# Feature-major products with a wider moving operand, and a 512-token job run inside the modulation's load

## What is computed

```python
# first block: x, ctx are 256 x 2048 each
sh, sc, gt = split(silu(c) @ w_ada + b_ada, 3)        # and the same of c_ctx
h_x = rms_norm(x, norm_g) * (1 + sc_x) + sh_x
h_c = rms_norm(ctx, norm_g) * (1 + sc_c) + sh_c
px, pc = split_cols(h_x @ w_in), split_cols(h_c @ w_in)   # w_in 2048 x 6976
# four attention mixers, w_out, x + gt_x * (...)
# second block
z, xbc, dt, q, k, v = split(rms_norm(h, g) @ w_in_2)      # xbc: 3072 columns
xbc = silu(causal_dwconv(xbc, conv_w))                    # 4 taps along the tokens
# state space and window attention, w_out_2
u = causal_dwconv(rms_norm(h, g) @ w_up, ffn_conv_w)      # 3 taps, 2 x 5632 columns
h = h + (silu(g_ff) * u_ff) @ w_down
# per-layer gate and projection
```

## Time and profile before

| | us |
|---|---|
| median of 3 runs | 2368.04 (2367.92 to 2368.23) |
| the profiled execution | 2368.59 |
| its span, first to last instruction | 2366.8 |
| TensorE busy | 2253.2 |
| VectorE busy | 1397.2 |
| ScalarE busy | 989.5 |

### The profile page before, as it was taken

One profiled execution on the slowest core, in us unless ns is written; L12 is line 12 of the kernel. 1 busy time (PEld: TensorE's weight loads), 2 busy tenths in 40 slices (PEclk: granted clock), 3 DMA queues, 4 the chain that ended last, 5 costly groups with the idle time before them and its releaser, 6 DMA issues.

```text
span 2366.8 us, 33302 instructions
## 1 busy us (share of the span) xinstructions
PE 2253.2 (95%) x13134; PEld 1927.9 (81%) x13134; DVE 1397.2 (59%) x1955; ACT 989.5 (42%) x1413; POOL 110.8 (5%) x106
## 2 busy tenths in 40 slices
PE   5899999998799899999989999999999999999998
PEld 1387888996568788998759888899999999788877
DVE  1357565634745577676566544667767776544465
ACT  1333232334544444444456544444444443344453
POOL 1000000002300021000000000000000000000000
PEclk8999999999899999999989999999999999999999
DMA  9975565543025466556400466556565665666554
GB/s 367 348 217 167 186 213 169 152 128 93 1 71 187 138 187 192 175 183 199 142 1 1 147 202 195 149 174 186 178 194 169 185 184 165 205 194 192 194 165 164
DMA packets 209084, 399.86 MB, mean 169 GB/s; under 512 B 15257, under 2 KB 23965, under 8 KB 208012
## 3 DMA queue, kind: packets, MB, share of 16 engines
q1 hardware_dynamic: 205520, 386.71, 51.9%
q0 software_dynamic: 2160, 7.20, 1.3%
q10 hardware_dynamic: 1292, 4.41, 0.5%
HBM read 395.25 MB, written 3.01 MB: 168 GB/s over the span
## 4 chain that ended last, share of the span: by engine, by line
PE 86%; DVE 6%; DMA 4%; ACT 2%; issue 1%; POOL 1%; SPq 0%; DVEq 0%; ACTq 0%
PE bank L1765 51%; PE bank L1776 27%; DMA ada_ring<-in_w_ada 4%; PE bank L1878 1%; PE bank L2046 1%; PE bank L1939 1%; PE bank L1861 1%; PE bank L1928 1%; PE bank L2059 1%; DVE wlo L1079 1%; PE bank L1870 0%; PE bank L1930 0%; POOL st L570 0%; PE bank L1905 0%; ACT kt L677 0%
## 5 line engine op out<-in xcount | busy, mean ns | idle before, releaser
L1079 DVE TENSOR_TENSOR wlo<-raw,whi 128x1024 fp32r<-128x1024 f32 (+2 forms) x649 | 773.5, 1204 | 584.7 <-ACT whi L670 570.3
L670 ACT ACTIVATE whi<-raw 128x1024 fp32r<-128x1024 f32 (+2 forms) x649 | 669.6, 1045 | 858.8 <-PE bank L1765 413.2
L1765 PE MATMUL bank<-whi,xl 128*128 128x512 f32 (+2 forms) x1904 | 734.0, 386 | 20.1 <-DVE wlo L1079 10.0
L1765 PE MATMUL bank<-whi,xh 128*128 128x512 f32 (+2 forms) x1904 | 728.4, 383 | 0.0
L1765 PE MATMUL bank<-wlo,xh 128*128 128x512 f32 (+2 forms) x1904 | 728.2, 382 | 0.0
L1776 PE MATMUL bank<-xl,whi 128*128 128x256 f32 x1792 | 507.9, 283 | 0.3 <-DVE xl L1128 0.3
L1776 PE MATMUL bank<-xh,wlo 128*128 128x256 f32 x1792 | 507.3, 283 | 0.0
L1776 PE MATMUL bank<-xh,whi 128*128 128x256 f32 x1792 | 507.2, 283 | 0.0
L1765 PEld LDWEIGHTS bank<-whi,xl 128*128 128x128 f32 x1904 | 359.1, 189 | 93.9 <-DVE wlo L1079 12.5
L1765 PEld LDWEIGHTS bank<-wlo,xh 128*128 128x128 f32 x1904 | 359.2, 189 | 68.7
L1765 PEld LDWEIGHTS bank<-whi,xh 128*128 128x128 f32 x1904 | 359.3, 189 | 65.7
(11 more groups left out here) (310 smaller groups left out, 1570.5 us busy)
## 6 DMA issues: line engine op xcount, KB each, us to landing
raw<-in_w_in SPq DMA_DIRECT2D x216, 512.0 KB, 4.4
raw<-in_w_up SPq DMA_DIRECT2D x176, 512.0 KB, 3.7
raw<-in_w_out SPq DMA_DIRECT2D x96, 512.0 KB, 4.6
raw<-in_w_down SPq DMA_DIRECT2D x88, 512.0 KB, 4.8
ada_ring<-in_w_ada SPq DMA_DIRECT2D x64, 512.0 KB, 11.6
gate_w<-in_w_ada SPq DMA_DIRECT2D x32, 512.0 KB, 3.9
raw<-in_w_ple_gate SPq DMA_DIRECT2D x32, 512.0 KB, 4.9
raw<-in_w_in SPq DMA_DIRECT2D x16, 384.0 KB, 3.3
```

Source lines behind the costliest of these rows:

```text
L670: nc.scalar.activation(whi[:, slot, 0:size], raw[:, slot, 0:size], ACT.Copy).then_inc(hi_ready, 1)
L1079: tt_(wlo[:, slot, 0:size], raw[:, slot, 0:size], whi[:, slot, 0:size].bitcast(F32), ALU.subtract).then_inc(lo_ready, 1)
L1765: ins = mm(b4[tt][:, 0:width], x[:, o:o + P], w, start=k == 0 and i == 0, stop=k == last and i == 2)
```

## The change

It has four parts.

**Wide feature-major products.** `XH` and `XL` are now the two halves of one tensor `XHL`. One matmul has `whi` as stationary operand and both 256-token halves moving (512 columns, two pieces 15360 floats apart), and fills the whole bank: high x high in the first half, high x low in the second. A second one adds low x high to the second half. ACT copies the second half of each bank (`low_half`, `UX` for the up projection), DVE adds the first half (`whole`) and releases the banks; the taps read the sum in SBUF. The parts stand a step later in the lists. For `xbc` the first tap goes to ACT.

**Input tiles inside the modulation's load.** Jobs 0 and 1 change places: job 0 is now one with 24 products a tile. Its first six tiles are loaded after modulation tiles 8, 10, 24, 26, 40 and 42, split at 13, 14, 29, 30, 45 and 46, and multiplied after 18, 23, 34, 39, 50 and 55. Behind the load come two tiles of job 1, the last two of job 0, and the rest in order. The ring of modulation tiles has nine slots, outside the weight ring, and one bank.

**Rounds untied from tiles.** PE transposes for four rounds after modulation tiles 14, 15, 17 and 18 (and 16, 32 later), two banks in turn; ACT and DVE finish them after 16 to 19. The column products move from tile 18 to tile 15. x and ctx are loaded ahead of the gain rows, and x is normalised ahead of ctx.

**Gate tiles and the tail.** The first eight gate tiles move to every second tile of 16 to 30 (jobs 2 and 3, 12 products a tile). Behind the up projection ACT splits nine tiles before its last high part, and DVE has a split between each two parts.

The core of the diff:

```diff
-ADA_RING = 12
+ADA_RING = 9
...
+        XHL = at("xhl", 12288, [P, 2, 15360], FR)
+        XH, XL = XHL[:, 0, :], XHL[:, 1, :]
...
-        MOD = at("mod_rows", 35840, [P, 2 * D])
-        ADA = at("ada_ring", 0, [P, ADA_RING, 1024])
+        MOD = at("mod_rows", 35840, [P, 4, W])
+        ADA = [at(f"ada_ring{i}", o, [P, 1024]) for i, o in enumerate(
+            (24576, 25600, 26624, 37888, 38912, 39936, 40960, 41984, 49984))]
...
+        UX = at("up_x", 51032, [P, 4, 256])
...
-        X_ROUND = {27 + 2 * k + 6 * (k // 4): k for k in range(12)}
-        MOD_COLS = {16 * i + 18: i for i in range(3)}
+        MOD_COLS = {16 * i + 15: i for i in range(3)}
+        X_ROUND = {16 * (k // 4) + 16 + k % 4: k for k in range(12)}
+        X_TURN = {16 * (k // 4) + (14, 15, 17, 18)[k % 4]: k for k in range(12)}
+        IN1_LOAD = {16 * (k // 2) + (8, 10)[k % 2]: k for k in range(6)}
+        IN1_SPLIT = {16 * (k // 2) + 13 + k % 2: k for k in range(6)}
+        IN1_TILE = {16 * (k // 2) + (18, 23)[k % 2]: k for k in range(6)}
+        IN1_ORDER = ([(0, g) for g in range(6)] + [(1, 0), (1, 1), (0, 6), (0, 7)] + [(1, g) for g in range(2, 8)]
+                     + [(jj, g) for jj in range(2, 15) for g in range(8)])
 
...
-        def ada_bank(j):
-            return bank[0] if j % 2 == 0 else bank[4]
-
-        GATE_AT = {n: g for g, n in enumerate(8 * jj + i for jj in (1, 4, 5, 8) for i in range(8))}
+        GATE_AT = {n: g for g, n in enumerate([16, 18, 20, 22, 24, 26, 28, 30]
+                                              + [8 * jj + i for jj in (4, 5, 8) for i in range(8)])}
 
         def round_bank(r):
 
+            if r < R_KV:
+                return bank[6 + r % 2]
             return bank[((4, 5, 6, 7) if R_UP <= r < R_PP else (2, 3, 6, 7))[r % 4]]
...
+                if n in IN1_LOAD:
+                    load_tile(IN1_LOAD[n], IN1_T[0][IN1_LOAD[n]])
 
...
-            act.dma_start(CROW[0:16, :], a["c"].rearrange("a (k p) -> (a k) p", p=P)).then_inc(s_rows, 16)
-            act.dma_start(CROW[16:32, :], a["c_ctx"].rearrange("(k p) -> k p", p=P)).then_inc(s_rows, 16)
+            act.dma_start(H0N[:, :, :], a["x"][0].rearrange("(t p) n -> p t n", p=P)).then_inc(s_x, 16)
+            act.dma_start(CX[:, :, :], a["ctx"][0].rearrange("(t p) n -> p t n", p=P)).then_inc(s_xc, 16)
...
                     act.wait_ge(ada_used, n + 1)
-                    copy(MOD[:, col:col + W], ada_bank(j)[:, :]).then_inc(evac, 1)
+                    if j >= 4:
+                        act.wait_ge(s_modc, j // 2 - 1)
+                    copy(MOD[:, j % 4, :], bank[4][:, :]).then_inc(evac, 1)
...
-            split(0)
-            split(1)
+                if n in IN1_SPLIT:
+                    split(IN1_SPLIT[n])
+            split(6)
             act.wait_ge(s_bb, 4)
+            one_round(R_X, 12)
+            one_round(R_X, 13)
+            split(7)
+            one_round(R_X, 14)
+            one_round(R_X, 15)
+            split(8)
+            split(9)
...
+                        ins = copy(XBC[:, (c - 2048) // P + i, :], b[i][:, 256:512])
+                    ins.then_inc(low_copied, 1)
...
+            def low_half(b4, used):
+
+                act.wait_ge(tile_used, used)
+                for f in range(4):
+                    ins = copy(UX[:, f, :], b4[f][:, 256:512])
+                ins.then_inc(low_copied, 1)
+
             for n in range(N_UP + 2, N_UP + 16):
                 if n < N_UP + 10:
                     one_round(R_UP, n - N_UP - 2)
                 split(n)
-                if n == N_UP + 14:
+                if n == N_UP + 9:
+                    low_half(GB, N_UP + 8)
...
-                    if k == 7:
+                    if k == 1:
+                        act.wait_ge(g_ready, i + 1)
+                        low_half(UB, i * 16 + (N_UP + 16))
...
+                    if k == 9:
+                        low_half(GB, i * 16 + (N_UP + 24))
...
-            for n in range(N_DN, N_DN + 4):
+            for n in range(N_DN, N_DN + 9):
                 split(n)
+                if n == N_DN + 1:
+                    low_half(UB, N_DN)
...
+                if back == 3:
+                    dve.wait_ge(low_copied, q + 1)
+                    for i in range(4):
+                        x = XBC[:, 4 * q + i, :]
+                        ins = tt_(x, banks_of(j)[i][:, 0:256], x, ALU.add)
+                    own(ins)
+                    dve.sem_inc(evac, 1)
+                if back in (5, 6, 7):
...
+            def whole(b4, count):
+
+                dve.wait_ge(low_copied, count)
+                for f in range(4):
+                    ins = tt_(UX[:, f, :], b4[f][:, 0:256], UX[:, f, :], ALU.add)
+                own(ins)
+                dve.sem_inc(evac, 1)
+
...
+                        after_up(i, k - 2)
                     if k == 8:
                         low_product(i, i * 1024 + 4096)
-                    if 9 <= k <= 12:
-                        after_gate(i + 1, i * 16 + (N_UP + 24), GB, k - 9)
+                    if 9 <= k <= 13:
+                        after_gate(i + 1, k - 10)
             own.leave(10)
             split(N_DN)
+            split(N_DN + 1)
+            after_up(10, -1)
             for part in range(6):
-                after_up(10, N_DN, UB, part)
-                if part in (1, 3, 4):
-                    split(N_DN + 1 + (1, 3, 4).index(part))
+                split(N_DN + 2 + part)
+                after_up(10, part)
+            split(N_DN + 8)
             low_product(10, 14336)
 
             def later_dn(j, back):
                 if j == J_DN and back == 3:
                     one_round(R_PP, 0)
 
-            phase(N_DN + 2, N_PP, add_h(J_DN), later_dn)
+            phase(N_DN + 2, N_PP, add_h(J_DN), later_dn, begin=N_DN + 9)
...
                         o = c * W + f * P
-                        for i, (w, x) in enumerate(((whi, XL), (whi, XH), (wlo, XH))):
-                            ins = mm(b4[f][:, 0:256], w[:, slot, o:o + P], x[:, k * 256:(k + 1) * 256],
-                                     start=k == 0 and i == 0, stop=k == last and i == 2)
+                        mm(b4[f][:, :].rearrange("p (s n) -> p s n", s=2), whi[:, slot, o:o + P],
+                           XHL[:, :, k * 256:(k + 1) * 256], start=k == 0, stop=False)
+                        ins = mm(b4[f][:, 256:512], wlo[:, slot, o:o + P], XH[:, k * 256:(k + 1) * 256],
+                                 start=False, stop=k == last)
                 return ins
 
...
+                if 2 <= r < R_KV:
+                    pe.wait_ge(xl_ready, r - 1)
+                elif r >= 4:
...
+            def in1_tile(n):
+
+                jj, g = IN1_ORDER[n]
+                pe.wait_ge(xl_ready, R_X + 2 * g + 2)
+                tile(n, n % RING, lambda: token_major(banks_of(J_IN1 + jj), JOBS1[jj][2], 2, 2 * g, KD - 1, 512, 0, 512,
+                                                      n % RING))
...
-                j, slot = n // 8, ada_slot(n)
-                if n % 8 == 0 and j >= 2:
-                    pe.wait_ge(evac, j - 1)
+                j, slot = n // 8, n % ADA_RING
...
                     k = 2 * (n % 8) + c
                     q = 32 * (k % 4)
-                    ins = mm(ada_bank(j)[q:q + 32, :], CT32[:, k, :], ADA[:, slot, c * W:(c + 1) * W],
+                    ins = mm(bank[4][q:q + 32, :], CT32[:, k, :], ADA[slot][:, c * W:(c + 1) * W],
                              start=k < 4, stop=k >= KD - 4)
...
+                if n == 15:
                     pe.wait_ge(s_cols, 1)
+                if n in X_TURN:
+                    if X_TURN[n] == 0:
+                        pe.wait_ge(xn_ready, 1)
+                    one_round(R_X, X_TURN[n])
                 if n in MOD_COLS:
                     mod_columns(MOD_COLS[n])
-                if n in X_ROUND:
-                    if X_ROUND[n] == 0:
-                        pe.wait_ge(xn_ready, 1)
-                    one_round(R_X, X_ROUND[n])
-            jobs(N_IN1, J_IN1, IN1_T, 512, 0, nts=[j[2] for j in JOBS1])
+                if n in IN1_TILE:
+                    in1_tile(IN1_TILE[n])
+            one_round(R_X, 12)
+            one_round(R_X, 13)
+            mod_columns(3)
+            pe.wait_ge(evac, J_IN1)
+            pe.wait_ge(s_bb, 4)
+            in1_tile(6)
+            one_round(R_X, 14)
+            one_round(R_X, 15)
+            for n in range(7, 16):
+                in1_tile(n)
+            jobs(16, J_IN1 + 2, IN1_T[2:], 512, 0, nts=[j[2] for j in JOBS1[2:]])
```

## The result

The changed kernel takes **2347.3 us** (median of 6 runs, 2345.5 to 2350.8), the kernel before beside it 2368.0: a ratio of 0.9917, with a 95% interval of 0.9906 to 0.9929. It is faster by 20.7 us. The forecast was 42.4 us, and its range ended at 2345. The profiled execution took 2345.9 us with a span of 2344.0, 22.8 under the span before.

A forecast was written before the change was run, and what follows sets the result against it. TensorE, busy 95% of the span, was taken as the bound. Gains 23.8 + 3.8 + 18.8 - 4.0 = 42.4 us took the profiled 2368.59 to 2326.2, and the median, 0.55 lower, to 2325.6 us; range 2312 to 2345.

The forecast's parts named there:

- Part 1: Feature-major products: one fixed part of 13.3 ns less in each of 1792 groups, a gain of 23.8 us.
- it becomes 226.8 + 120.0: Feature-major group: one 512-column plus one 256-column matmul take 346.8 ns, where three narrow ones took 360.0.
- rival b: Feature-major products: the two-piece operand costs two fixed parts, or the fixed part stays; gain 0, 2349.4 us; chance 0.06.
- The cover: Feature-major job ends: copies, adds and split take 4.4 us within TensorE's 5.55 us of ready work, so cost nothing.
- rival (d): Feature-major job ends: copies, adds and split exceed 5.55 us, TensorE stands at 28 joins; 2394 us at 8 us; chance 0.04.
- Part 2: Tail of the up projection: TensorE's three waits for the split behind the last convolution vanish, a gain of 3.8 us.
- Part 3: Input projection in the modulation's load: 156 products done earlier, 35.4 us less 16.6, a gain of 18.8 us.
- The wait of 1.9: Modulation's load: rounds with two banks make TensorE wait for the first rounds' split, 1.9 us lost per period.
- without its last rounds: Modulation's load: the third period omits its last rounds and bank copy, taking 25.1 us instead of 26.9.
- Part 4: Gate tiles in 12-product jobs: two 750 ns VectorE steps each where VectorE is full, a loss of 4 us.
- The sentence on the SP queue behind a late gate step: Gate tiles: a late step holds up the SP queue, whose next load waits for the slot; no separate size.
- rival (a): Start: modulation tiles don't pair or hand-overs come later, gain there 2.6 us or less; 2341.8 us; chance 0.18.

The follow-up runs named there:

- e1: Changed kernel with the wide feature-major matmul split again, so three matmuls of 256 columns a group; 2362.2 us.
- e11: Changed kernel with every feature-major matmul 512 columns wide, the low weights also multiplying both input halves; 2525.4 us.
- e2: Changed kernel with the wide matmul reading 512 columns in one piece, not the reference's product; 2347.6 us.
- e3: Changed kernel with the wide matmul reading two pieces 512 floats apart, not the reference's product; 2347.1 us.
- e10: Changed kernel with feature-major loops exchanged, bank by bank: a tile's two wide matmuls, then its two narrow ones; 2337.0 us.
- e5: Changed kernel with modulation tiles 17, 33 and 49 multiplied twice more ahead of TensorE's wait, so modulation is wrong; 2341.0 us.
- e6: Changed kernel with third and fourth rounds behind tiles 19 and 20, input tiles one place later, the sixth behind the load; 2339.4 us.
- e13: Changed kernel with moved start and four wide, four narrow matmuls, then gate tiles 1 to 7 cut to 16 columns; 5885.5 us, not used.
- e12: Changed kernel with moved start and four wide, four narrow matmuls, then gate loads issued by ScalarE instead of SyncE; 2334.6 us.
- e9: Changed kernel with moved start and four wide, four narrow matmuls, then first eight gate tiles beside 24-product tiles only; 2373.8 us.

## Why the prediction was right or wrong

**Part 1, forecast 23.8, measured 11.4 to 11.8.** The mechanism was right: one fixed part of 13.3 ns less in each group, and e1, e11 show it at both widths in this form of product. The step that failed is "it becomes 226.8 + 120.0": the two rows came from stretches of one width, and I added them for a stretch that alternates. That costs 6.6 ns a group, 1792 x 6.6 = 11.8 us, nearly half the forecast. I had looked for the doubt in the operand's two pieces (rival b), where e2 and e3 show none. The bounds of 0 to 71.7 held it, but I took the nearest row as if it were exact. The cover was right too: PE is at 100% in both stretches, and rival (d) didn't come.

The sentence from the Trainium skill (TensorE: Matmul & The Clock Gate, section Back-to-back issue gap) gave 4.5 us for this part. By that rule one instruction less saves an estimated 2.5 ns a group; from e1 to e10 it is 11.6 (360.0 to 348.4). Its result of 2344.9 lies near the measured one by luck, not for its reason.

**Part 2, forecast 3.8, measured 4.2** for all that lies behind the up projection. No wait of PE is left behind the up projection; the chain runs on in one piece there:

```profile
1987.14 59.86 PE bank L1841 x264
```

**Part 3, forecast 18.8, measured 11.0.** PE is free of the start at 142.6 (the piece below), forecast 134.8. The steps behind the last column products took 10.97 us against 11.0, so the miss is all in the periods: 29.1, 29.9 and 27.2 for 26.9, 26.9 and 25.1, 7.3 us, and 0.5 at the first. The wait of 1.9 was priced nearly right (2.22, 2.41 and 2.40). The step that failed is that all of a period's work was priced at full clock. In the three stretches at 0.50 (6.8, 6.8 and 3.4 us) PE is busy for 4.58, 5.59 and 3.03 us; half of that, 6.6 us in all, is my estimate of what the clock cost. A smaller slip is the third period "without its last rounds": the diff has rounds 12 and 13 ahead of the last column products, and they take 0.9 us there (130.72 to 131.65). With 1.3 us of longer waits that is more than the 7.3, so other terms were priced a little high. I had the warning in the earlier trace rows: 12 products took 4.58 us after 3 us of idling, and I used it only for the gain. e5 shows that the fall goes away when PE's work ahead of the wait is longer and the wait short, and e6 that the wait itself was avoidable and that a shorter fall comes without it. What exactly makes the clock fall is not shown.

```profile
142.62 27.50 PE bank L1841 x120
```

**Part 4, forecast -4, measured -5.5** by PE's idle time, within its bounds of 1 to 8. The mechanism, DVE's steps in a full stage, is borne out by e13 (steps cut, 5.2 us less) and by e12 (the queue freed, nothing less). The sentence on the SP queue behind a late gate step was true of the trace and of no weight here.

The sum of the parts as measured is 11.4 + 4.2 + 11.0 - 5.5 = 21.1 against 22.8 in the spans; the rest is the +2.9 and -1.3 of the stretches between. So two steps failed, by 12 and 8 us, and both in the same direction. The range ended at 2345 because it took in only one miss at a time; rival (a) alone gave 2341.8, and half of (b) on top of half of (a) gives 2345.6, near where the kernel landed.

## What to carry to other kernels

A pace read from a uniform stretch holds for a uniform stretch: where a change makes widths alternate, group equal widths in runs (two by two gave back 5.0 of the 6.6 ns) before counting on it. Where light matmuls (column products of 2 columns and products with 32 output partitions here) stand around a wait of 2 us, price the work there at half the clock for some us, or put other ready work in the wait's place, and look at the granted clock again: e6 still had short falls. And a late load or a long queue wait in the trace proves nothing until the engine that is full there has been ruled out: e12 took 36 us of such waiting away and gained nothing, while e9, where the trace shows the same queue holding up everybody, was 40 us slower.

## What the runs showed of the hardware

- Matmuls of 512 and 256 columns in turn take 353.4 ns a pair where the two widths alone give 346.8; in runs of two 348.4, four 350.8, eight 349.1. Bank and distance of the operand's pieces make no difference.
- One instruction with two pieces of 256 columns, 15360 floats apart, runs at the pace of 512 adjacent columns (226.7 ns).
- The granted clock fell to 0.50 from 48.0 to 54.8 us, around a 2.2 us idle of TensorE that began at 48.6, behind 16 column products (2 columns each) and 8 matmuls of 32 output partitions. It did not fall with the run ahead made longer and the idle 0.7 us (e5), and fell for 3.4 us with no idle there (e6).
